# State outputs in four column quarters, mLSTM gate rows transposed beside the second chunk, NSA weights between second and third chunk

## The chip, the cores and the metric

One core of one Trainium2 chip runs the whole program in one launch. The metric is the time on the device in microseconds, the median of several runs. The other seven cores do nothing.

## The reference, cut to what matters

The program is two layers on 256 tokens of width 2048, all float32. The first layer has three branches: stick-breaking attention (8 heads), an S5 state space layer (64 groups, here 8 blocks of four state tiles) and an mLSTM (4 heads), then a mixture of 32 experts. The second layer has an RG-LRU branch, NSA attention (8 heads) and a forgetting attention. Three pieces bear on the change.

```python
# S5: the output of the states, 8 groups' 128 channels per block
y = einsum('bsgp,ghp->bsgh', states, c_mat).real + d_skip * u
# mLSTM: gates per head and token, used by row and by column
log_f = log_sigmoid(f_pre); b = cumsum(log_f)
log_d = b[t] - b[s] + log_i[s]
# NSA: probabilities of softmaxes over keys, then the values
p = masked_softmax(q @ k.T * scale, mask)
o = gate * (p @ v)
```

## The kernel before, in words

Activations lie with channels on the 128 partitions and the 256 tokens along the free axis. Every weight matrix comes in chunks of one megabyte (128 x 2048 floats). SyncE issues their loads into four buffers `stage`. ScalarE copies a chunk to `w_hi` (fp32r), GpSimd computes the rest `w_lo` = stage - w_hi in four pieces of 512 columns (L549), and TensorE (`chunk`, `wide`) multiplies: 32 matmuls with w_hi, then 16 with w_lo, into bank k of `acc`, chunk n using bank n mod 4. GpSimd's `low` for chunk n waits until chunk n - 2 is done, for `w_lo` has two buffers. `wide` takes a function `mid` that is called between the 32 and the 16 matmuls, and that is where small products of an earlier head are put. `opening` multiplies the first tiles of a projection whose last tile isn't computed yet, `closing` the rest. `evac_done` counts the evacuations of acc.

The engines run their own programs and meet in semaphores only; the order of work on each is the order in the code. Loops over heads are software pipelined: iteration i projects head i (g) and computes head i - 1 (s).

`stage_a` (attention and S5). Its projections are `plain`: 32 fp32 records from `stage` directly, chunks 0 to 3 giving q, k, v, u; a function passed in is called ahead of t = 11 of 16. A product in fp32 is two records of TensorE. Around them stand the scores and transposes of v; `bu(j)`, the input of state tile j into bank 2 of `wk`, for j = 0 to 3; `sums`; `values`; and `cmm(j)`, the product of the rotated states of tile j with their output matrix `A_cm`, 32 output channels, which go to partitions 32j to 32j + 31 of bank 3 of `wk`. On VectorE, `rotate(j)` turns bu(j) into the states: t1 and t2 from bank 2, vr, two scans (A_sc), t1 and t2 again, and `srot`; its two buffers are reused, so rotate(2) and (3) wait for cmm(0) and (1). The order on VectorE is rotate(0), sp, rotate(1), the argument of w, rotate(2), the mask of w, rotate(3), yl, y5 (which waits for the last cmm), then `tables` of the next head, from which ScalarE computes sine and cosine. GpSimd has no work in this stage until its end. After the eighth head the first chunks of projection p_sb are opened beside what is left of it; their w_hi are copied by ScalarE behind the softplus of the eighth head.

`ada_part` multiplies 512 columns by 32 columns in each of four quarters of the array, as the expert stage (`up_step`, `down`) does with four experts.

mLSTM gates. Chunk `mlif` gives the gates of all heads; ScalarE evacuates them, converts one more w_hi and computes abs, exp, ln; VectorE follows with six steps (row_d 1 to 6) on four partitions. TensorE waits for them (L835), transposes rows to columns (L837), waits for `row_done`, and runs the eight chunks of head 0 (`stage_b(0, None)`, beside which no head's products stand). ScalarE waits for `row_t` ahead of its part of stage_b.

`stage_c` (NSA, one RG-LRU block beside each head) has four chunks per head. TensorE runs `scores`, chunk 0, chunk 1 with `probs` as its mid, chunk 2 with `values` as its mid, chunk 3. `probs` begins with `sums` of the next head, then waits for the scaled weights of VectorE (c_d, C_P) and transposes them (L1142, L1144); ScalarE copies the transposed ones to SBUF (C_pT, C_pcT) for `values`.

Of the kernel before, what the change touches and what calls it, by code (L numbers as in the profile page):

```python
# [22 lines left out]
P = 128  # L23
T = 256
# [84 lines left out]
def build(nc, dr):  # L109
# [37 lines left out]
    M0 = D0 + 32768  # L147
# [35 lines left out]
    A = {}  # L183
# [5 lines left out]
    for n, s in [("ph", [P, 4, T]), ("sin", [P, 4, T]), ("cos", [P, 4, T]), ("t1", [P, 2, T]), ("t2", [P, 2, T])]:  # L189
        A[n] = ar("A_" + n, s)  # L190
    ar = Area(S0, END)
    for n, s in [("y5", [P, WT, T]), ("vr", [P, 2, T]), ("sc", [P, 2, T]), ("srot", [P, 2, 2, T]),
                 ("craw", [P, 4, 2, 32]), ("cm", [P, 4, 2, 32]), ("c1", [P, 4, 2, 32]), ("c2", [P, 4, 2, 32]),
                 ("mask", [P, 2, T]), ("iota", [P, T]), ("s5p", [P, 14, 32])]:
        A[n] = ar("A_" + n, s)
    ar = Area(S0 + 8192, S0 + 8192 + 6144)
# [368 lines left out]
    def _(pe):  # L565
# [179 lines left out]
        def stage_a(g, s):  # L745
# [10 lines left out]
            def cmm(j):  # L756
                rs = slice(32 * j, 32 * j + 32)
                pe.wait_ge(srot_ready, s * 4 + j + 1)
                mm(wk[rs, 3, 0:T], A["cm"][:, j, 0, :], A["srot"][:, j % 2, 0, :], True, False)
                mm(wk[rs, 3, 0:T], A["cm"][:, j, 1, :], A["srot"][:, j % 2, 1, :], False, True)\  # L760
                    .then_inc(cmm_done, 1)
# [34 lines left out]
            if s is not None:  # L796
                pe.wait_ge(vtok_ready, s + 1)
                cmm(0)
                bu(2)
            if g is not None:  # L800
                plain(2, g)
            else:
                opening("p_sb", 2, 7)
            if s is not None:
                cmm(1)
                bu(3)
                values()
            beside_plain(3, g, s, lambda: cmm(2))
            if s is not None:
                cmm(3)  # L810
# [24 lines left out]
        pe.wait_ge(row_d, 6)  # L835
        for st in range(2):
            last = pe.transpose(wk[:, 0, 4 * st:4 * st + 4], B["g"][0:4, st * P:(st + 1) * P], ident[0:4, 0:4])  # L837
        last.then_inc(row_t, 1)
        pe.wait_ge(row_done, 1)
        base_b = BASE["ml"]  # L840

        def stage_b(g, s):
# [18 lines left out]
            for j in range(8):  # L861
                if g is not None:
                    wide(*slot(base_b + j, g, 2))
                elif j < 4:
                    opening("p_ml", j, 6)
# [12 lines left out]
        stage_b(0, None)  # L878
        with pe.Fori(1, 4) as i:
            stage_b(i, i - 1)  # L880
# [228 lines left out]
        def stage_c(g, s, kv):  # L1109
# [26 lines left out]
            def probs():  # L1136
                if g is not None:
                    sums()
                pe.wait_ge(c_d, s * NC_D + (C_FIRST + C_P))
                for i in range(2):  # L1140
                    for st, tt in ((0, 0), (0, 1), (1, 1)):
                        pe.transpose(wk[:, i, (st + tt) * P:(st + tt + 1) * P], C["z"][:, 2 * i + tt, st * P:(st + 1) * P], ident[:])  # L1142
                for tt in range(2):
                    last = pe.transpose(wk[0:16, tt, 384:512], C["zc"][:, tt, :], ident[:])  # L1144
                last.then_inc(c_p, 1 if g is not None else 2)
# [23 lines left out]
            beside(base_c + 1, g, s, probs, "p_a", 1)  # L1169
# [671 lines left out]
    def _(dve):  # L1841
# [156 lines left out]
        def stage_a(g, s):  # L1998
# [20 lines left out]
            def rotate(j):  # L2019
# [23 lines left out]
                if j >= 2:  # L2043
                    dve.wait_ge(cmm_done, s * 4 + j - 1)
                tt(A["srot"][:, j % 2, 0, :], A["t1"][:, 0, :], A["t2"][:, 1, :], SUB)
                tt(A["srot"][:, j % 2, 1, :], A["t2"][:, 0, :], A["t1"][:, 1, :], ADD).then_inc(srot_ready, 1)
# [17 lines left out]
            dve.wait_ge(cmm_done, s * 4 + 4)  # L2064
# [817 lines left out]
```

## Time and profile before

| | us |
|---|---|
| median of 3 runs | 3269.16 (3265.61 to 3270.73) |
| profiled execution, on the device | 3263.18 |
| its span | 3261.4 |
| TensorE busy | 2918.5 (89%) |
| GpSimd busy | 1677.4 (51%) |
| VectorE busy | 1270.4 (39%) |
| ScalarE busy | 1183.5 (36%) |
| mean granted TensorE clock | 0.957 of full speed |

Rows of the profile name an engine (PE is TensorE, PEld its weight load, DVE VectorE, ACT ScalarE, POOL GpSimd, SP SyncE), a line of the kernel, the operation and the tiles (written <- read). Starts are in microseconds from the span's start. A bracket such as [1.63 <-DVE C_rq] is idle time of the engine just before, and what ended it. Matmuls overlap: the time of a merged row runs to the end of its last record, and the next row begins before that. Most lines are those of helpers (L567 is `mm`, L1843 VectorE's `tt`, L1287 ScalarE's `fn`), so groups are told apart by their tiles. The heads of stage_a lie between 130 and 415 us, the mLSTM gates at 820, the NSA heads between 2172 and 2415.

### The profile page before, as it was taken

To read this page: it belongs to the slowest core of one execution; us is meant where nothing else is said; L and a number is where in the kernel's file an instruction comes from. 1 tells how busy PE (TensorE), PEld (TensorE's weight loads), DVE (VectorE), ACT (ScalarE), POOL (GpSimd) and SP (SyncE) were. 2 spreads that over 40 slices of the span, in tenths; PEclk is the share of its full clock that TensorE was granted. 3 is DMA by queue.
4 is the path that set the end of the run, shared out by engine and by line. 5 is a ranking of instruction groups with operands and counts; after the bars stand their busy time and mean duration, and the time that the engine had idled before them with its cause. 6 is when DMAs were issued, how large, how long until landed. Compare 5 with 4: busy or idle time off the path is not lost.

```text
span 3261.4 us, 51720 instructions
## 1 busy us (share of the span) xinstructions
PE 2918.5 (89%) x20048; PEld 2413.4 (74%) x20048; DVE 1270.4 (39%) x2025; ACT 1183.5 (36%) x1378; POOL 1677.4 (51%) x1274
## 2 busy tenths in 40 slices
PE   6899979999899999857788768979999999999998
PEld 1677767787898878733344427879988989999998
DVE  1477742214363252331222214436633153324335
ACT  1222233333445332310111104546554446654343
POOL 0000047677677676400000003966669997769798
PEclk8999989999999999978999988989999999999999
DMA  9533337558344586659777893543335554445444
GB/s 390 205 109 109 109 112 287 199 217 296 133 151 158 182 305 249 223 209 414 328 321 314 333 420 148 191 140 138 132 131 193 182 195 155 154 142 193 158 168 142
DMA packets 98628, 679.77 MB, mean 208 GB/s; under 512 B 11584, under 2 KB 15424, under 8 KB 16832
## 3 DMA queue, kind: packets, MB, share of 16 engines
q1 hardware_dynamic: 83088, 602.97, 49.4%
q10 hardware_dynamic: 15408, 74.85, 6.1%
q8 instruction: 106, 1.74, 0.2%
q14 instruction: 26, 0.21, 0.0%
HBM read 770.05 MB, written 2.10 MB: 237 GB/s over the span
## 4 chain that ended last, share of the span: by engine, by line
PE 70%; DMA 12%; DVE 6%; ACT 5%; issue 3%; POOL 2%; ACTq 1%; SPq 1%; DVEq 0%; POOLq 0%
PE acc L567 42%; PE wk L567 11%; PE acc L640 9%; DMA ring<-in_moe 6%; PE acc L644 5%; DMA side_buf<-in_ada 3%; POOL w_lo L549 2%; DMA stage<-in_ada 2%; PE acc L653 2%; ACT L1287 1%; ACT w_hi L1287 1%; DVE C_z L1846 1%; DMA stage<-in_main 1%; SPq L499 1%; ACT hb L1287 0%
## 5 line engine op out<-in xcount | busy, mean ns | idle before, releaser
L549 POOL TENSOR_TENSOR w_lo<-stage,w_hi 128x512 fp32r<-128x512 f32 x1268 | 1670.2, 1351 | 1535.3 <-ACT w_hi L1287 1014.3
L1287 ACT ACTIVATE w_hi<-stage 128x2048 fp32r<-128x2048 f32 x317 | 603.8, 1907 | 47.9 <-DMA stage<-in_main 47.5
L567 PE MATMUL acc<-xhl,w_hi 128*128 128x256 f32 x4064 | 525.2, 288 | 21.9 <-DVE xhl L1843 9.8
L567 PEld LDWEIGHTS acc<-xhl,w_hi 128*128 128x128 f32 x4064 | 509.2, 196 | 25.9 <-DVE xhl L1843 6.8
L640 PE MATMUL acc<-xhl,w_hi 128*128 128x512 f32 x1536 | 371.3, 394 | 0.0
L640 PEld LDWEIGHTS acc<-xhl,w_hi 128*128 128x128 f32 x1536 | 281.6, 188 | 92.7 <-issue 37.7
L567 PE MATMUL acc<-xhl,w_lo 128*128 128x256 f32 x2032 | 274.6, 289 | 2.0 <-POOL w_lo L549 2.0
L567 PEld LDWEIGHTS acc<-xhl,w_lo 128*128 128x128 f32 x2032 | 259.3, 196 | 5.5 <-issue 2.5
L567 PE MATMUL acc<-h,stage 128*128 128x256 f32 x1024 | 232.8, 384 | 2.9 <-ACT h L1287 2.9
L567 PEld LDWEIGHTS acc<-h,stage 128*128 128x128 f32 x1024 | 193.5, 191 | 38.3 <-issue 12.8
L567 PE MATMUL acc<-ring,xg 128*32 128x512 f32 x1024 | 145.2, 712 | 73.0 <-DMA ring<-in_moe 72.3
L644 PEld LDWEIGHTS acc<-xhl,w_lo 128*128 128x128 f32 x1536 | 196.9, 191 | 7.5
L644 PE MATMUL acc<-xhl,w_lo 128*128 128x256 f32 x1536 | 199.1, 283 | 0.0
L1287 ACT ACT_TABLE_LOAD x137 | 175.8, 1283 | 51.3 <-DVE G_sg L1843 27.4
L567 PEld LDWEIGHTS acc<-ring,xg 128*32 128x32 f32 x1024 | 41.5, 128 | 170.8 <-issue 169.9
L567 PE MATMUL acc<-yh,w_hi 128*128 128x256 f32 x576 | 141.6, 284 | 5.2 <-DVE yl L1843 5.2
L567 PE MATMUL acc<-yl,w_hi 128*128 128x256 f32 x576 | 141.2, 283 | 0.0
L567 PE MATMUL acc<-dh,w_hi 128*128 128x256 f32 x512 | 127.2, 289 | 6.4 <-DVE dl L1843 6.4
L567 PE MATMUL acc<-dl,w_hi 128*128 128x256 f32 x512 | 125.3, 285 | 0.0
L1843 DVE TENSOR_TENSOR X_hid<-X_s,acc 128x256 f32<-128x256 f32 (+1 forms) x12 | 5.0, 418 | 297.3 <-ACT X_s L1287 297.3
L567 PEld LDWEIGHTS acc<-yh,w_hi 128*128 128x128 f32 x576 | 109.8, 191 | 5.5 <-DVE yl L1843 3.6
L567 PEld LDWEIGHTS acc<-dh,w_hi 128*128 128x128 f32 x512 | 98.6, 193 | 19.3 <-issue 16.2
(485 smaller groups left out, 4054.2 us busy)
## 6 DMA issues: line engine op xcount, KB each, us to landing
stage<-in_main SPq DMA_DIRECT2D x317, 1024.0 KB, 4.8
ring<-in_moe SPq DMA_DIRECT2D x192, 1024.0 KB, 10.4
side_buf<-in_ada ACTq DMA_DIRECT2D x64, 1024.0 KB, 5.0
over_lo<-in_moe ACTq DMA_DIRECT2D x48, 1024.0 KB
over_hi<-in_moe ACTq DMA_DIRECT2D x42, 1024.0 KB
stage<-in_ada SPq DMA_DIRECT2D x32, 1024.0 KB, 8.6
stage<-in_sb SPq DMA_DIRECT2D x32, 1024.0 KB, 4.8
x<-in_x ACTq DMA_DIRECT2D x1, 2048.0 KB, 12.9
```

What stands on the lines that cost most here:

```text
L499: sp.dma_start(ring[:, r, :], dr["moe"][tile * 6 + c]).then_inc(ring_in[r], 16)
L549: last = pool.tensor_tensor(w_lo[:, k % 2, cs], stage[:, k, cs], w_hi[:, k, cs].bitcast(F32), ALU.subtract)
L567: return pe.matmul(o, w, r, start=start, stop=stop)
L640: pe.matmul(acc[:, k, :], w_hi[:, k, t * P:(t + 1) * P], xhl[:, :, t, :], start=t == 0, stop=False, skip_group_check=True)
L644: last = pe.matmul(acc[:, k, 0:T], w_lo[:, k % 2, t * P:(t + 1) * P], xh[:, t, :], start=False, stop=t == DT - 1, skip_group_check=True)
L653: return pe.matmul(o, w, r, start=start, stop=stop, skip_group_check=True)
L1287: return act.activation(o, i, f, **kw)
L1843: return dve.tensor_tensor(o, a, b, op)
L1846: return dve.tensor_scalar(o, a, s1, s2, op0, op1) if op1 else dve.tensor_scalar(o, a, s1, None, op0)
```

## The change

1. `cmm` is one block of eight matmuls for all four tiles, with the quarter j running fastest, called ahead of t = 11 of the fourth projection (or in the middle of the fourth opening), after a wait for all four rotations. `srot` has four buffers (the two new ones lie where sq1 was), so rotate waits for no cmm. `bu(3)` moves from behind the third projection into it, and y5 waits for cmm_done s + 1.
2. `columns` (the wait for the gate rows and their two transposes) is the mid of the second mLSTM chunk; the wait for row_done is behind all eight chunks of head 0.
3. In stage_c `sums` is the mid of chunk 1 by itself, and `probs` stands between chunks 1 and 2.

```diff
--- before.py
+++ after.py
@@ -188,11 +188,13 @@
     ar = Area(M0, S0)
     for n, s in [("ph", [P, 4, T]), ("sin", [P, 4, T]), ("cos", [P, 4, T]), ("t1", [P, 2, T]), ("t2", [P, 2, T])]:
         A[n] = ar("A_" + n, s)
+    srots = [None, None, sb("A_srot2", [P, 2, T], at=M0), sb("A_srot3", [P, 2, T], at=M0 + 2048)]
     ar = Area(S0, END)
     for n, s in [("y5", [P, WT, T]), ("vr", [P, 2, T]), ("sc", [P, 2, T]), ("srot", [P, 2, 2, T]),
                  ("craw", [P, 4, 2, 32]), ("cm", [P, 4, 2, 32]), ("c1", [P, 4, 2, 32]), ("c2", [P, 4, 2, 32]),
                  ("mask", [P, 2, T]), ("iota", [P, T]), ("s5p", [P, 14, 32])]:
         A[n] = ar("A_" + n, s)
+    srots[0], srots[1] = A["srot"][:, 0], A["srot"][:, 1]
     ar = Area(S0 + 8192, S0 + 8192 + 6144)
     for n, s in [("y5sg", [P, 2, 2 * T]), ("sg", [P, 2, T])]:
         A[n] = ar("A_" + n, s)
@@ -753,12 +755,14 @@
                 mm(wk[:, 2, 0:T], A["bcur"][rs, 0, :], A["u"][rs, :])
                 mm(wk[:, 2, T:2 * T], A["bcur"][rs, 1, :], A["u"][rs, :]).then_inc(bu_done, 1)
 
-            def cmm(j):
-                rs = slice(32 * j, 32 * j + 32)
-                pe.wait_ge(srot_ready, s * 4 + j + 1)
-                mm(wk[rs, 3, 0:T], A["cm"][:, j, 0, :], A["srot"][:, j % 2, 0, :], True, False)
-                mm(wk[rs, 3, 0:T], A["cm"][:, j, 1, :], A["srot"][:, j % 2, 1, :], False, True)\
-                    .then_inc(cmm_done, 1)
+            def cmm():
+
+                pe.wait_ge(vtok_ready, s + 1)
+                pe.wait_ge(srot_ready, s * 4 + 4)
+                for c in range(2):
+                    for j in range(4):
+                        last = mm(wk[32 * j:32 * j + 32, 3, 0:T], A["cm"][:, j, c, :], srots[j][:, c, :], c == 0, c == 1)
+                last.then_inc(cmm_done, 1)
 
             if s is not None:
                 pe.wait_ge(sb_evac, s * 4 + 7)
@@ -794,20 +798,11 @@
                 bu(1)
             beside_plain(1, g, s, sums)
             if s is not None:
-                pe.wait_ge(vtok_ready, s + 1)
-                cmm(0)
                 bu(2)
-            if g is not None:
-                plain(2, g)
-            else:
-                opening("p_sb", 2, 7)
+            beside_plain(2, g, s, lambda: bu(3))
             if s is not None:
-                cmm(1)
-                bu(3)
                 values()
-            beside_plain(3, g, s, lambda: cmm(2))
-            if s is not None:
-                cmm(3)
+            beside_plain(3, g, s, cmm)
 
         heads(pe, stage_a)
 
@@ -832,11 +827,13 @@
 
         each(pe, BASE["mlif"], 1, wide)
         ada_columns(3, side_row[1])
-        pe.wait_ge(row_d, 6)
-        for st in range(2):
-            last = pe.transpose(wk[:, 0, 4 * st:4 * st + 4], B["g"][0:4, st * P:(st + 1) * P], ident[0:4, 0:4])
-        last.then_inc(row_t, 1)
-        pe.wait_ge(row_done, 1)
+
+        def columns():
+            pe.wait_ge(row_d, 6)
+            for st in range(2):
+                last = pe.transpose(wk[:, 0, 4 * st:4 * st + 4], B["g"][0:4, st * P:(st + 1) * P], ident[0:4, 0:4])
+            last.then_inc(row_t, 1)
+
         base_b = BASE["ml"]
 
         def stage_b(g, s):
@@ -860,7 +857,7 @@
                 last.then_inc(bvt_done, 1)
             for j in range(8):
                 if g is not None:
-                    wide(*slot(base_b + j, g, 2))
+                    wide(*slot(base_b + j, g, 2), mid=columns if j == 1 and s is None else None)
                 elif j < 4:
                     opening("p_ml", j, 6)
                 if j == 1 and s is not None:
@@ -876,6 +873,7 @@
                     last.then_inc(num_done, 1)
 
         stage_b(0, None)
+        pe.wait_ge(row_done, 1)
         with pe.Fori(1, 4) as i:
             stage_b(i, i - 1)
         pe.wait_ge(by_ready, 3)
@@ -1134,8 +1132,6 @@
                 last.then_inc(c_p, 1)
 
             def probs():
-                if g is not None:
-                    sums()
                 pe.wait_ge(c_d, s * NC_D + (C_FIRST + C_P))
                 for i in range(2):
                     for st, tt in ((0, 0), (0, 1), (1, 1)):
@@ -1166,7 +1162,11 @@
                 wide(*slot(base_c, g))
             else:
                 opening("p_a", 0, 7)
-            beside(base_c + 1, g, s, probs, "p_a", 1)
+            if g is not None:
+                wide(*slot(base_c + 1, g), mid=sums)
+            else:
+                opening("p_a", 1, 7)
+            probs()
             beside(base_c + 2, g, s, values, "p_a", 2)
             if g is not None:
                 wide(*slot(base_c + 3, g))
@@ -2040,10 +2040,8 @@
                 tt(A["t1"][:], A["sc"][:], cos, MUL)
                 tt(A["t2"][:], A["sc"][:], sin, MUL).then_inc(vo_ch, 1)
                 dve.wait_ge(vo_ch, done.next())
-                if j >= 2:
-                    dve.wait_ge(cmm_done, s * 4 + j - 1)
-                tt(A["srot"][:, j % 2, 0, :], A["t1"][:, 0, :], A["t2"][:, 1, :], SUB)
-                tt(A["srot"][:, j % 2, 1, :], A["t2"][:, 0, :], A["t1"][:, 1, :], ADD).then_inc(srot_ready, 1)
+                tt(srots[j][:, 0, :], A["t1"][:, 0, :], A["t2"][:, 1, :], SUB)
+                tt(srots[j][:, 1, :], A["t2"][:, 0, :], A["t1"][:, 1, :], ADD).then_inc(srot_ready, 1)
 
             rotate(0)
 
@@ -2061,7 +2059,7 @@
             rotate(3)
             dve.wait_ge(yh_ready, s + 1)
             tt(yl[:, s, :], wk[:, 0, 0:T], yh[:, s, :].bitcast(F32), SUB).then_inc(yl_ready, 1)
-            dve.wait_ge(cmm_done, s * 4 + 4)
+            dve.wait_ge(cmm_done, s + 1)
             tt(A["y5"][:, s, :], wk[:, 3, 0:T], A["du"][:], ADD).then_inc(y5_ready, 1)
             done.check()
             if g is not None:
```

## Rows read from the trace of the kernel before

**Rows 1.** the page, part 1 (busy, share, count) and part 4 (chain)
```profile
PE 2918.5 (89%) x20048; PEld 2413.4 (74%) x20048; DVE 1270.4 (39%) x2025; ACT 1183.5 (36%) x1378; POOL 1677.4 (51%) x1274
...
PE 70%; DMA 12%; DVE 6%; ACT 5%; issue 3%; POOL 2%; ACTq 1%; SPq 1%; DVEq 0%; POOLq 0%
```

**Rows 2.** waits of TensorE, whole span: total us, times, longest
```profile
PE acc L653 <- ACT w_hi L1287: 12.9, 1, 12.9
...
PE wk L1142 <- DVE C_rq L1846: 11.6, 7, 1.8
...
PE wk L837 <- DVE B_rows L1849: 10.6, 1, 10.6
...
PE wk L567 <- DVE A_t L1843: 3.2, 6, 0.5
...
PE wk L1142 <- DVE C_zc L1846: 0.7, 1, 0.7
```

**Rows 3.** timeline of TensorE in a head: start, us, what, count
```profile
370.04 1.05 PE L567 MATMUL wk<-A_srot,A_cm 128*32 128x256 f32 x4
...
371.02 2.43 PE L567 MATMUL acc<-h,stage 128*128 128x256 f32 x10
```

**Rows 4.** timeline of VectorE in the heads
```profile
342.25 0.69 DVE L1843 TENSOR_TENSOR A_t<-wk,A_cos 128x512 f32<-128x512 f32 x1 [0.17 <-ACT A_cos L1287]
...
364.34 0.69 DVE L1843 TENSOR_TENSOR A_t<-wk,A_cos 128x512 f32<-128x512 f32 x1 [2.86 <-PE wk L567]
...
369.20 0.76 DVE L1843 TENSOR_TENSOR A_srot<-A_t,A_t 128x256 f32<-128x256 f32 x2
...
374.55 0.42 DVE L1843 TENSOR_TENSOR A_y<-wk,A_du 128x256 f32 x1 [4.25 <-PE wk L567]
...
415.34 0.42 DVE L1843 TENSOR_TENSOR A_y<-wk,A_du 128x256 f32 x1 [4.26 <-PE wk L567]
```

**Rows 5.** timeline of TensorE behind the heads
```profile
430.44 0.55 PE L653 MATMUL acc<-yh,w_hi 128*128 128x256 f32 x1 [12.89 <-ACT w_hi L1287]
...
459.23 1.05 PE L567 MATMUL wk<-A_srot,A_cm 128*32 128x256 f32 x4
```

**Rows 6.** timeline of TensorE: quarters in ada_part, and in the experts
```profile
806.11 1.06 PE L567 MATMUL wk<-side_buf,cact 128*32 128x512 f32 x8 [0.58 <-DMA side_buf<-in_ada]
...
1702.99 3.64 PE L567 MATMUL acc<-ring,xg 128*32 128x512 f32 x32
```

**Rows 7.** timeline of TensorE around the mLSTM gates
```profile
819.74 0.95 PE L567 MATMUL wk<-ident,side_row 128*128 128x4 f32 x8
...
831.32 0.37 PE L837 MATMUL wk<-ident,B_rg 4*128 4x4 f32 x2 [10.63 <-DVE B_rows L1849]
...
839.13 4.00 PE L567 MATMUL acc<-xhl,w_hi 128*128 128x256 f32 x32
...
842.97 2.08 PE L567 MATMUL acc<-xhl,w_lo 128*128 128x256 f32 x16
```

**Rows 8.** timeline of VectorE there: the gate chain's first step
```profile
828.22 0.41 DVE L1849 SCALAR_TENSOR_TENSOR B_rlf<-B_rlf,B_rl 4x256 f32<-4x256 f32 x1 [7.31 <-ACT B_rl L1287]
```

**Rows 9.** timeline of GpSimd there
```profile
839.44 5.48 POOL L549 TENSOR_TENSOR w_lo<-stage,w_hi 128x512 fp32r<-128x512 f32 x4 [14.46 <-PE acc L567]
```

**Rows 10.** windows: busy (count) by engine, granted clock, DMA share, GB/s
```profile
825.00:830.00 5.00, 0.00 (x0) 0.00 (x0) 1.68 (x4) 3.08 (x4) 0.00 (x0) 0.50 0.64 210
```

**Rows 11.** tile B_rm: duration ns min/median/max, first and last start
```profile
L1846 DVE TENSOR_SCALAR B_rm<-B_rows,ident x4: 470/1508/1508, 862.4 to 1034.3; 4x512 f32<-4x512 f32 x4
```

**Rows 12.** timeline of TensorE in an NSA head
```profile
2281.63 0.50 PE L567 MATMUL wk<-ones,C_qs 128*128 128x1 f32 x4
...
2283.75 0.88 PE L1142 MATMUL wk<-ident,C_z 128*128 128x128 f32 x6 [1.63 <-DVE C_rq L1846]
...
2290.43 0.59 PE L567 MATMUL wk<-C_pT,C_vtok 128*128 128x256 f32 x2
```

**Rows 13.** timeline of ScalarE there
```profile
2284.88 0.81 ACT L1287 ACTIVATE C_pT<-wk 128x768 f32<-128x768 f32 x1 [0.58 <-PE wk L1144]
```

## Prediction

> **What bounds the kernel now.** I read the page's busy times and chain first: TensorE is busy 89% of the span and carries 70% of the chain that ended last [rows 1]. So a microsecond is won where TensorE has less to do or stops waiting, and the list of TensorE's waits says where it waits [rows 2]. Five of its lines belong to the three places of this change: 3.2 us in six waits on A_t, one of 12.9 us on w_hi behind the heads, one of 10.6 us on B_rows ahead of the mLSTM chunks, 11.6 us in seven waits on C_rq and one of 0.7 us on C_zc in the NSA heads. That is 39 us of waiting, besides the work that the first edit packs closer. Then I read the timelines around each.
>
> **State outputs in quarters (stage_a).** Removed on TensorE: the four separate cmm blocks of a head. One block is two fp32 matmuls, four records, from 370.04 to 371.02: 0.98 us [rows 3], which is 4 x 0.216 (ten of the next kind take 2.43 to the end of the last) and a switch of 0.1. Added: one block of eight matmuls, 16 records, in which four neighbours go to four column quarters. What do neighbours in different quarters cost? The trace has them: ada_part's eight records of 512 columns (four quarters, twice) take 1.06 us to the end of the last, and 32 such records in the expert stage 3.64 us; the 24 more cost 2.58, 0.107 us each, where a record of 512 columns by itself needs 2 x 0.216 = 0.43 [rows 6]. Four run at once. With 256 columns a round of four costs 0.216, and the new block has four rounds: 0.87 + 0.1 = about 0.98 us. The bounds: 0.98, and serial 16 x 0.216 + 0.1 = 3.56. I take 0.98, since ada_part is the same form. The Trainium skill ("TensorE: Matmul & The Clock Gate", measured speedup) gives three column tiles a speedup of 2.38 and four row tiles 3.07, not 4. By 3.07, an estimate, the block would cost 1.2 and the sum below would be 1.8 us smaller; the expert row, at its full fourfold rate, speaks against it.
>
> Three blocks fewer in a head is 2.94 us. From the first full head to the end of the last projection of the eighth, 27 old blocks become 7 new ones: 20 x 0.98 = 19.6 us. What could eat it is the new wait for all four rotations, behind which the last ten projection matmuls, the next scores and everything else on TensorE queue up. Before, the last rotation ran 364.34 to 369.96 (5.62 us), after VectorE had sat idle 2.86 us for the fourth bu [rows 4]. That bu moves ahead of the end of the third projection, so VectorE no longer waits and the rotation ends at 367.1. TensorE gets to the place of the new block at 370.04 less two old blocks, 368.1: 1.0 us to spare, and more later, since y5 (before at 374.55) now follows at 369.2 and the tables with it. The 0.53 us wait on A_t goes too: rotation 0 begins 8.5 us after y5 (342.25, where the y5 before it was at 333.76, one period of 40.79 us ahead of 374.55; the period is 415.34 less 374.55, [rows 4]), reads its product by 379.0 (two steps, 0.69 us each, [rows 4]), and TensorE asks for that at 380.9 (before at 383.9; three blocks, 2.94, earlier). 6 waits: 3.2 us. The loads of the next S5 matrices (ScalarE's queue, behind the values' evacuation and the fourth bu) come forward with both; stage's projection loads are a megabyte each in 9 us or more. No new wait there. VectorE's own loop from y5 to y5 is 8.5 + 4 x 5.6 + 2.6 for the three mask steps + 1.1 = 34.6 us under a period of 37.3.
>
> The end of the heads: y5 of the seventh head at 415.34 [rows 4] starts tables, sine, softplus, the copies of w_hi, and TensorE begins p_sb at 430.44 after 12.9 us idle [rows 5]. That chain now starts 2.35 us before the end of the last projection instead of 0.98 us behind it: 3.3 us less idle. Then the openings, counted from the first one's start: the first takes 7.5 us, bu 1 1.0, the second with sums 6.5, and without cmm 0 bu 2 ends at 16.1. Rotation 2 and the mask step end at 22.3; the third opening (3.3) with bu 3 inside ends at 20.4, so values wait 1.9 us and end at 23.4. Rotation 3 ends at 27.9; half of the fourth opening (1.7) is done at 25.1, so the block waits 2.7 and ends at 28.9, and the other half at 30.5. Before, all was done 0.98 us behind 459.23, at 29.8 from 430.44 [rows 5]: 0.7 us lost. Behind it the GpSimd w_lo chain starts at the first closing and moves along. Part one: 19.6 + 3.2 + 3.3 - 0.7 = 25.4 us.
>
> **mLSTM gate columns (columns).** Before: ada_columns end at 820.65 (819.74 + 0.9), TensorE is idle to 831.32, transposes, waits for row_done, has chunk 0 issued at 839.13 and chunk 1 at 844.9 (842.97 and 16 x 0.12) [rows 7]: 24.3 us. The granted clock fell to 0.50 in the idle, the 1.2 GHz level [rows 10], and so chunk 0 took longer than chunk 1's 5.76 us. After: chunk 0 (5.76), the first 32 of chunk 1's 48 matmuls (3.84, from 839.13 to 842.97 before), then the wait at 830.25. The gate chain on ScalarE and VectorE is unmoved and would be ready at 831.3, a wait of 1.0. But now a GpSimd w_lo of four pieces, that began at 839.44 when chunk 0 was done [rows 9], begins at 826.6 and lies over the VectorE chain, six steps from 828.22 on [rows 8]. What such overlap costs, a step on four partitions shows: 0.47 us alone, 1.51 beside GpSimd [rows 11]. Between nothing and 0.9 us on each step; the w_lo ends about 832.0, so the chain ends about 833.6: wait 3.3 us. The Trainium skill ("GPSIMD Engine Reference", key points) names this contention for VectorE instructions with two SBUF inputs or in a 2-port mode; by it both scans suffer as well, which changes nothing as w_lo's end limits it. After the wait: transposes and switches 0.4, last 16 matmuls 1.95; end 835.9. Gain 9.0 us (between 8, when the clock falls in the wait, and 11.3, with no contention). ScalarE stands in its wait for row_t, so chunk 0's evacuation and the next w_hi come at 834 instead of 826.8; that w_hi is for chunk 4, wanted at 845 or later. row_done, now behind eight chunks, is free. A stage buffer is released by w_lo, not by this, so loads hold.
>
> **NSA weights (stage_c).** Before: sums at 2281.63, then an idle of 1.63 us, the transposes of C_z at 2283.75 [rows 12]. After: sums 0.36 at the same place, then the chunk's 16 w_lo matmuls (1.95), then the transposes at about 2284.05; VectorE's weights were ready at 2283.70. The wait is gone with 0.3 us to spare; the extra switch costs 0.1. The values need ScalarE's copies: they begin at 2284.88 [rows 13], take 0.81 and a small one, and end some 1.3 us behind the transposes, and TensorE now gets to values 3.84 us behind them instead of 5.8 (2290.43, [rows 12]): held. Chunk 1 is done 2.5 us earlier, so its w_lo partner lies over VectorE's LRU steps, perhaps 3 us longer; those are wanted only after values, and the next conv starts at the third chunk's evacuation, 8 us off. Gain 7 x (1.66 - 0.1) = 10.9, and 0.6 in the last head, where the 0.7 us on C_zc goes: 11.5.
>
> **Sum.** 25.4 + 9.0 + 11.5 = 45.9 us. The profiled execution took 3263.18 us on the device for a span of 3261.4, 6.0 under the median of the three runs, 3269.16; so 3217.3 for an execution like it, and 3223 against the median, which I forecast. What lies behind the three places moves as a block: the expert stage's ring loads are released by chunks, not by a clock of their own.
>
> **Rivals.**
> Quarters don't overlap in this form (the eight matmuls accumulate in one bank, two rounds over). For it: no row has 256 columns in quarters. Against: the expert rows accumulate round after round. Then 2.6 us more in each of seven heads: 3241. Chance 0.12.
> A wait only moves. In NSA the spare is 0.3 us; were VectorE's scaling a microsecond or two later, the wait would come back at the new place: 11 us kept, 3234. Chance 0.10. With the first case, or with the mLSTM gain lost too, 3250: 0.05.
> More than I count: no GpSimd overlap in the gate chain, a clock that holds through the openings: 3217 or a little less. Chance 0.10.
> The other side: VectorE's loop becomes the bound. All rotations now lie between cmm and cmm without overlap by the next y5. It decides from 37.3 us on (34.6 by rows), and makes the kernel slower only from about 43.7 us a head, that is with VectorE's steps a quarter longer; then 3276. For it: GpSimd overlap does such things. Against: GpSimd is idle in this stage. Chance 0.03.
> The change does nothing measurable (waits reappear in full, quarters serial): 3266, chance 0.04.
> The forecast itself: 0.56.
>
> **How the numbers follow.** The forecast's own bounds (the block 0.98 to 1.2, the gates 8 to 11.3, runs that spread by 5 us) give 3215 to 3230. With the serial and the NSA case the range is 3209 to 3245; beyond it are at most 0.12. A measurement of this kernel tells 0.2%, 6.5 us, from no change. Faster by more: 0.93; within: 0.04; slower: 0.03.
>
> **What would show it.** In the profile after: the x16 group wk<-A_srot,A_cm of about 1.1 us once a head with no idle before it; period 37.3; no wait on A_t; p_sb's opening about 26 us earlier; the L837 transposes behind an idle of 1 to 4 us and a clock of 1.00 in chunk 0; the L1142 transposes with no idle, and values with none. A block of 3.5 us, an idle ahead of it, or an idle ahead of the values would make it wrong.

## The result, and the profile after

The kernel after takes 3214.33 us (median of 4 runs, 3209.77 to 3221.9), beside 3268.67 for the kernel before in the same rounds: a ratio of 0.9839 with a 95% interval of 0.9823 to 0.9854, about 54 us less. Forecast were 3223 with a range of 3209 to 3245; the result lies in the range, and just below the forecast's own bounds of 3215 to 3230. The profiled execution took 3212.35 us on the device for a span of 3210.6, 50.8 less than the span of before, so the forecast of 3217.3 for such an execution was 5 us too high.

The page, parts 1 and 4, and then TensorE's waits over the whole span (total us, times, longest), those that answer to [rows 1, 2]:

```profile
PE 2891.5 (90%) x20048; PEld 2402.3 (75%) x20048; DVE 1291.0 (40%) x2025; ACT 1182.6 (37%) x1378; POOL 1682.0 (52%) x1274
...
PE 55%; DMA 9%; DVE 4%; ACT 2%; issue 2%; POOL 2%; SPq 1%; ACTq 1%; DVEq 0%; POOLq 0%
```

```profile
PE acc L655 <- ACT w_hi L1287: 10.8, 1, 10.8
...
PE wk L834 <- DVE B_rows L1849: 3.7, 1, 3.7
...
PE wk L569 <- DVE A_srot L1843: 2.7, 1, 2.7
...
PE wk L569 <- DVE A_w L1843: 1.5, 1, 1.5
```

TensorE has as many instructions as before and 27 us less busy time. Some 23.5 of them are the blocks: eight heads have three blocks of 0.98 us fewer each, since records in different quarters now lie over each other. The rest is not split up; the clock has a part in it, for matmuls at the lower clock are busy longer. The waits on A_t, C_rq and C_zc are gone, B_rows is 3.7 instead of 10.6. I cut the trace at TensorE instructions that both kernels have: heads are first to eighth scores (wk<-A_q,A_k), "to p_sb" from there to the first matmul on yh, "p_sb" from there to the next product of a side buffer, "gates" from the second transposes of side_row to the first product of B_qk, "NSA" first to eighth wk<-C_ks,C_q. The remainder is all else; most of it is stages that wait for loads, and it holds the eighth NSA head too. All in us (the difference is taken before rounding):

| kernel | heads | to p_sb | p_sb | gates | NSA | remainder | span |
|---|---|---|---|---|---|---|---|
| before | 284.9 | 15.3 | 72.4 | 63.9 | 223.4 | 2601.6 | 3261.4 |
| after | 259.5 | 13.1 | 73.5 | 58.0 | 208.0 | 2598.4 | 3210.6 |
| difference | 25.3 | 2.2 | -1.1 | 5.9 | 15.4 | 3.2 | 50.8 |

The heads of after. Timeline of TensorE, start, us, what, count; first a block of quarters one head earlier, then one with what is next to it:

```profile
349.76 1.07 PE L569 MATMUL wk<-A_srot,A_cm 128*32 128x256 f32 x16
...
386.83 1.07 PE L569 MATMUL wk<-A_srot,A_cm 128*32 128x256 f32 x16
387.83 2.43 PE L569 MATMUL acc<-h,stage 128*128 128x256 f32 x10
```

Sixteen records take 1.00 us from the block's start to the next row's, no idle is in front of them, and the period is 37.07 us. In before four records took 0.98, about the same [rows 3]. The block has room: on VectorE the last rotation of the first of these two heads ends at 347.65, 2.1 us ahead of the block, where 1.0 was forecast.

```profile
346.89 0.76 DVE L1843 TENSOR_TENSOR A_srot<-A_t,A_t 128x256 f32<-128x256 f32 x2
```

The gates. Timelines of TensorE, VectorE and GpSimd, then windows (length, then busy us and count of PE, PEld, DVE, ACT and POOL, then granted clock, DMA share, GB/s):

```profile
792.30 4.07 PE L569 MATMUL acc<-xhl,w_hi 128*128 128x256 f32 x32
...
798.12 4.00 PE L569 MATMUL acc<-xhl,w_hi 128*128 128x256 f32 x32
805.82 0.37 PE L834 MATMUL wk<-ident,B_rg 4*128 4x4 f32 x2 [3.69 <-DVE B_rows L1849]
806.12 3.78 PE L569 MATMUL acc<-xhl,w_lo 128*128 128x256 f32 x16
809.70 5.07 PE L569 MATMUL acc<-xhl,w_hi 128*128 128x256 f32 x32
```

```profile
799.98 1.28 DVE L1849 SCALAR_TENSOR_TENSOR B_rlf<-B_rlf,B_rl 4x256 f32<-4x256 f32 x1 [7.33 <-ACT B_rl L1287]
801.29 1.66 DVE L2116 TENSOR_TENSOR_SCAN B_rb<-ones,B_rlf 4x256 f32<-4x256 f32 x1
...
804.32 0.68 DVE L2120 TENSOR_TENSOR_SCAN B_rm<-ones,B_rg 4x256 f32<-4x256 f32 x1
```

```profile
798.44 5.58 POOL L551 TENSOR_TENSOR w_lo<-stage,w_hi 128x512 fp32r<-128x512 f32 x4 [1.59 <-PE acc L569]
```

```profile
800.00:803.00 3.00, 2.12 (x18) 1.92 (x16) 2.93 (x3) 0.00 (x0) 3.00 (x3) 1.00 0.38 161
803.00:806.00 3.00, 0.18 (x2) 0.18 (x2) 2.66 (x4) 0.00 (x0) 1.01 (x1) 0.88 0.31 44
806.00:809.00 3.00, 3.00 (x15) 2.98 (x15) 2.05 (x6) 2.18 (x2) 0.00 (x0) 0.50 0.73 309
809.00:812.00 3.00, 3.00 (x16) 3.00 (x15) 1.61 (x2) 2.07 (x2) 2.02 (x2) 0.50 0.02 5
```

Up to 804.0 GpSimd's w_lo lies over VectorE's chain: the first step takes 1.28 us where it took 0.41 [rows 8], and the scans are 1.66 beside GpSimd and 0.68 behind it. That makes most of the wait of 3.69 us (gates_hold, below). The Trainium skill ("GPSIMD Engine Reference", key points) names VectorE instructions with two SBUF inputs or in a 2-port mode for this contention. The scans and the first step have two, and the trace agrees. In gates_third a step that reads one tile, the TENSOR_SCALAR on B_rows, is drawn out too, from 0.28 to 1.20 us; whether it runs in such a mode no run shows. Behind the wait the clock is 0.50 for 6 us: 16 w_lo matmuls take 3.78 us, not the 2.08 of [rows 7], and the next 32 take 5.07, not 4.00.

NSA in after, timeline of TensorE: no idle ahead of the transposes, none ahead of the values.

```profile
2241.81 0.50 PE L569 MATMUL wk<-ones,C_qs 128*128 128x1 f32 x4
2242.17 2.15 PE L569 MATMUL acc<-xhl,w_lo 128*128 128x256 f32 x16
2244.16 0.82 PE L1138 MATMUL wk<-ident,C_z 128*128 128x128 f32 x6
...
2248.86 0.59 PE L569 MATMUL wk<-C_pT,C_vtok 128*128 128x256 f32 x2
```

### The profile page after: what moved, and what is told of

It is laid out like the page before. It is cut to its first block, busy times and chain, and to the rows that moved or that the text cites. A ratio compares the mean times of both kernels' runs of the same rounds, so it can differ in the third digit from the quotient of the medians.

```text
span 3210.6 us, 51704 instructions
## 1 busy us (share of the span) xinstructions
PE 2891.5 (90%) x20048; PEld 2402.3 (75%) x20048; DVE 1291.0 (40%) x2025; ACT 1182.6 (37%) x1378; POOL 1682.0 (52%) x1274
## 4 chain that ended last, share of the span: by engine, by line
PE 55%; DMA 9%; DVE 4%; ACT 2%; issue 2%; POOL 2%; SPq 1%; ACTq 1%; DVEq 0%; POOLq 0%
PE acc L569 35%; DMA ring<-in_moe 8%; PE wk L569 7%; PE acc L642 7%; PE acc L646 4%; POOL w_lo L551 2%; DMA side_buf<-in_ada 2%; PE acc L655 2%; ACT w_hi L1287 1%; SPq L501 1%; ACT hb L1287 0%; DVE hb L1843 0%; ACT L1287 0%; DMA stage<-in_main 0%; DVE dl L1843 0%
```

## The experiments

**Each edit alone.** The first three kernels have one part of the diff each, on top of the kernel before (the first is the change of `cmm`, `srots` and `stage_a`; the second that of the mLSTM `columns`; the third that of `stage_c`).

The core of each:

```diff
-            beside_plain(3, g, s, lambda: cmm(2))
-            if s is not None:
-                cmm(3)
+            beside_plain(3, g, s, cmm)
```

> The kernel before with the first edit alone (the one block in four quarters, bu(3) moved, four srot buffers). Theory: the block costs about 1.0 us and the A_t wait is gone, so a head takes 37.1 us instead of 40.8, the opening of p_sb comes 27 us earlier and the whole gains 25 to 28 us: 3241 to 3244 against 3268.7. Rival (a part of the gain is given back in the side-loaded stages behind, which wait for DMA): under 20 us in the whole, though the heads are 26 us shorter.

```diff
-                    wide(*slot(base_b + j, g, 2))
+                    wide(*slot(base_b + j, g, 2), mid=columns if j == 1 and s is None else None)
```

> The kernel before with the gate columns in the second mLSTM chunk alone. Prediction on record: 9.0 us. Theory from the two traces: TensorE's wait of 3.7 us is followed by about 6 us at the 1.2 GHz level, which costs 2.8 us, so the stretch from ada_columns to the first B_qk product is 5.9 us shorter and the whole gains 4 to 8 us. Rival: the clock fell in that one execution by chance; then here the wait is followed by a clock of 1.00 and the stretch is 8.7 us shorter.

```diff
-            beside(base_c + 1, g, s, probs, "p_a", 1)
+            if g is not None:
+                wide(*slot(base_c + 1, g), mid=sums)
+            else:
+                opening("p_a", 1, 7)
+            probs()
```

> The kernel before with the NSA edit alone. Prediction on record: 10.9 us for seven heads, 11.5 in all. Theory from the two traces: 1.76 us a head, and two heads of the kernel before (34.3 and 32.9 us instead of 31.2) lost 3.1 and 1.7 us more after their waits, by the clock, which goes too: heads of 29.5 us, 15 us in all. Rival: those two long heads have another cause and stay: 12.3 us in all.

| kernel | median, us | ratio to before (95%) | heads | to p_sb | p_sb | gates | NSA | remainder |
|---|---|---|---|---|---|---|---|---|
| p1_only | 3247.69 | 0.9934 (0.9917 to 0.9951) | 259.5 | 13.1 | 75.5 | 64.1 | 223.4 | 2604.9 |
| p2_only | 3262.37 | 0.9976 (0.9962 to 0.9990) | 284.8 | 15.3 | 72.0 | 57.6 | 223.4 | 2617.4 |
| p3_only | 3248.98 | 0.9937 (0.9918 to 0.9956) | 284.8 | 15.3 | 72.0 | 64.6 | 208.0 | 2603.3 |

Each edit moves its own stretch, by what it moves it in the whole change to 0.4 us, and no other (gates differ by up to 0.7 us without a cause known, and p_sb is in question to 3 us). Within that the parts are independent, as the sum assumed. In p2_only the wait of 3.69 us and the 3.78 us of w_lo behind it are there again, so the fall of the clock was no accident of one execution.

The whole times say less. Against the median of the kernel before in their rounds, 3269.61, p1_only is 21.9 us faster, where 25 to 28 were expected and its stretches give 24; p2_only is 7.2, within the 4 to 8 expected; p3_only is 20.6, where its stretch gives 15.4. The remainder, whose code is the same in all but for the eighth NSA head, lies between 2597 and 2617 us over thirteen profiled executions. A single edit of 6 us is read from its stretch, not from a median of a few runs (ten of p2_only, four of the others).

**Are the quarters at once, and what for?** Two kernels on top of after, one with another order of the block's matmuls, one with the block done twice:

```diff
-                for c in range(2):
-                    for j in range(4):
+                for j in range(4):
+                    for c in range(2):
```

> The changed kernel, with the eight state-output matmuls of a head in another order: both matmuls of a quarter one behind the other, then the next quarter, where the changed kernel goes through the four quarters and then once more. Theory: matmuls run at once only where neighbours in the stream are in different quarters. Then two records out of four have a neighbour of their own quarter ahead (each matmul being two records, half and half), the block of 16 records, 1.01 to 1.07 us in the changed kernel, takes from 2.0 us (pairs serial) to 3.5 us (all serial), the period of a head goes from 37.08 to 38.1 to 39.6 us, and the kernel becomes 7 to 20 us slower than the changed kernel's 3214. Rival: each matmul starts when its quarter is free, whatever stands in front of it, with its two halves already one behind the other in the same quarter: the block stays at about 1.0 us and the time at 3214.

```diff
-                for c in range(2):
+                for c in (0, 1, 0, 1):
```

> The changed kernel, with the eight state-output matmuls of a head done twice (the second pass starts the sums anew, so what is computed stays the same): 32 records where there were 16. Theory: four quarters at once and TensorE the bound of a head: the block goes from 1.01 to 1.07 us to 1.88 (0.87 more), the period of a head from 37.08 to 37.95, and the kernel from 3214 to 3221. Rival (VectorE's loop bounds the head by now, so that TensorE has slack behind the block): the block grows and the period stays at 37.1. Rival (quarters are partly serial and the short block hides it in a fixed share): the block goes to more than 2.2 us.

Timelines of TensorE, the first fence of the other order, the second of the doubled block:

```profile
386.26 1.09 PE L569 MATMUL wk<-A_srot,A_cm 128*32 128x256 f32 x16
387.28 2.43 PE L569 MATMUL acc<-h,stage 128*128 128x256 f32 x10
```

```profile
356.35 1.93 PE L569 MATMUL wk<-A_srot,A_cm 128*32 128x256 f32 x32
...
394.30 1.93 PE L569 MATMUL wk<-A_srot,A_cm 128*32 128x256 f32 x32
396.16 2.43 PE L569 MATMUL acc<-h,stage 128*128 128x256 f32 x10
```

Then two windows of the other order, of the block's records alone (length, busy and count of TensorE, clock, DMA share, GB/s):

```profile
386.26:386.32 0.06, 0.06 (x4) 1.00 0.00 0
386.32:386.48 0.16, 0.16 (x4) 1.00 0.00 0
```

The first theory, that only neighbours in different quarters overlap and the block takes 2.0 to 3.5 us, fell; its rival held. With all four records of a quarter one behind another the block takes 1.02 us from start to start, 0.02 more, and the heads 259.7 us instead of 259.5 (3218.71 us, ratio 0.9847, 0.9827 to 0.9866). So the matmuls needn't alternate between quarters within 16 records. The windows show how it starts: four records within the first 0.06 us, and no fifth up to 0.22. The trace doesn't name the quarter of a record. But records of one quarter alone started 0.216 us apart in before [rows 3], so the four are most likely in four quarters, and three of them then began ahead of earlier records of a busy quarter. How TensorE does that is not shown.

The doubled block takes 1.86 to 1.87 from start to start, 0.87 more as expected: four more rounds of 0.216. The period is 37.95, so the block is on the path to the full and VectorE's loop has at least 0.9 us to spare. The heads are 265.6 us, 6.0 more, about 7 x 0.87 (3223.79 us, ratio 0.9875, 0.9857 to 0.9894).

**The gates: what makes the wait, and what the clock?** Three kernels on top of after. The first puts the transposes one chunk later:

```diff
-                    wide(*slot(base_b + j, g, 2), mid=columns if j == 1 and s is None else None)
+                    wide(*slot(base_b + j, g, 2), mid=columns if j == 2 and s is None else None)
```

> The kernel after with the gate columns as the mid of the third mLSTM chunk instead of the second. Theory: TensorE comes to the columns 5.8 us later, when the rows are ready or nearly so, so the 3.7 us wait goes and with it the low clock behind it (2.8 us): 5 to 6.5 us shorter from ada_columns to the first B_qk product than in the kernel after. Rival (ScalarE, which stands in its wait for the columns, becomes late with the w_hi of the fifth chunk): a new wait on w_hi of 1 us or more at the fifth chunk, and a gain under 4 us.

The second holds GpSimd back until the six VectorE steps are done:

```diff
-        each(pool, 4, BASE["kv"] - 4, low)
+        each(pool, 4, BASE["ml"] + 2 - 4, low)
+        pool.wait_ge(row_d, 6)
+        each(pool, BASE["ml"] + 2, BASE["kv"] - BASE["ml"] - 2, low)
```

> The changed kernel, with the first low-part subtraction of the third mLSTM chunk on GpSimd held until the six VectorE steps of the gate chain are done. Theory: the wait of 3.7 us on B_rows is GpSimd's contention with VectorE's steps, and the clock of 0.50 behind it comes of the wait: with GpSimd held the steps take about 0.3 to 0.7 us each as before the change, the wait is about 1.0 us, the clock stays at 1.00, the 16 low matmuls behind it take 2.08 instead of 3.78 and the high ones 4.00 instead of 5.07: the stretch from the gates' side row to the first B_qk matmuls goes from 58.0 to about 52.5 to 53 us. The third chunk's low part is then ready at about 5.6 us behind the end of the chain, 0 to 1 us ahead of TensorE's need. Rival (the steps wait for something else than GpSimd, ScalarE's chain say): the wait stays at 3 us or more and the clock falls again. Rival (the wait moves): a new wait of 1 to 4 us on w_lo at the third chunk, and the stretch ends where it was.

The third leaves GpSimd and the wait as they are and keeps TensorE occupied ahead of it:

```diff
         def columns():
+            for _ in range(14):
+                mm(wk[:, 0, T:T + P], ones[:], ident[:])
             pe.wait_ge(row_d, 6)
```

> The changed kernel with 14 extra 128-column matmuls (ones by the identity, into a part of the bank that nobody reads; some 3.0 us in all) on TensorE right ahead of its wait for the gate rows, of 3.7 us in the changed kernel. The wait itself stays. Theory: the clock of 0.50 behind the wait comes of TensorE standing idle; filled, the idle is 0.7 us, the clock stays at 1.00, the 16 low matmuls behind it take 2.1 us instead of 3.78 and the next 32 take 4.0 instead of 5.07, and the stretch from the side row to the first B_qk matmuls goes from 58.0 to 55.3. Rival: the clock falls for another reason (the load on the other engines at that time, or a fixed moment of the program): the low matmuls stay at 3.78, the stretch at 58.0.

gates_hold, timeline of VectorE, then of TensorE:

```profile
802.32 0.41 DVE L1851 SCALAR_TENSOR_TENSOR B_rlf<-B_rlf,B_rl 4x256 f32<-4x256 f32 x1 [7.32 <-ACT B_rl L1289]
802.77 0.68 DVE L2118 TENSOR_TENSOR_SCAN B_rb<-ones,B_rlf 4x256 f32<-4x256 f32 x1
803.48 0.41 DVE L1845 TENSOR_TENSOR B_rg<-B_rli,B_rb 4x256 f32<-4x256 f32 x1
```

```profile
805.42 0.28 PE L836 MATMUL wk<-ident,B_rg 4*128 4x4 f32 x2 [0.95 <-DVE B_rows L1851]
805.63 2.18 PE L571 MATMUL acc<-xhl,w_lo 128*128 128x256 f32 x16
```

gates_filled, timeline of TensorE, then a window of it:

```profile
804.57 3.29 PE L569 MATMUL wk<-ident,ones 128*128 128x128 f32 x28
808.43 0.28 PE L836 MATMUL wk<-ident,B_rg 4*128 4x4 f32 x2 [0.57 <-DVE B_rows L1851]
808.64 2.18 PE L569 MATMUL acc<-xhl,w_lo 128*128 128x256 f32 x16
```

```profile
806.00:809.00 3.00, 2.43 (x22) 2.22 (x21) 2.44 (x5) 0.20 (x1) 0.63 (x1) 1.00 0.24 82
```

| kernel | wait on B_rows | w_lo x16 behind it | gates | median, us | ratio to before (95%) |
|---|---|---|---|---|---|
| after | 3.69 | 3.78 | 58.0 | 3214.33 | 0.9839 (0.9823 to 0.9854) |
| gates_third | 0.85 | 2.18 | 52.4 | 3216.46 | 0.9842 (0.9817 to 0.9866) |
| gates_hold | 0.95 | 2.18 | 53.5 | 3213.44 | 0.9844 (0.9823 to 0.9866) |
| gates_filled | 0.57 | 2.18 | 55.3 | 3217.7 | 0.9842 (0.9821 to 0.9862) |

gates_hold: with GpSimd held, all six steps are at their short durations and the wait is 0.95 instead of 3.69 us. GpSimd's overlap makes 2.7 us of the wait. The rival that the wait would move is right for a part, though not at w_lo. The first product of B_qk comes 1.1 us later than in gates_third, since it waits 2.75 us for ScalarE's evacuation and not 1.77. ScalarE's w_hi copies ahead of it wait 2.2, 2.0, 3.3 and 1.4 us for loads, where those of gates_third don't; that the stage buffers come free later behind the held w_lo is the likely reason, not tested. Another 1.5 us goes behind that product (170.4 us from the first to the fourth, 168.9 in every other kernel), and the trace says on what: behind the idle of 2.75 us the clock is 0.50 and the eight matmuls take 3.43 us, behind the one of 1.77 it is 1.00 and they take 1.99. Timeline and window, first of gates_hold, then of gates_third:

```profile
847.35 3.43 PE L571 MATMUL wk<-B_qk 128*128 128x256 f32 x8 [2.75 <-ACT B_qk L1289]
847.00:849.00 2.00, 1.65 (x4) 1.38 (x5) 0.00 (x0) 1.58 (x2) 1.31 (x2) 0.50 0.38 160
...
843.15 1.99 PE L569 MATMUL wk<-B_qk 128*128 128x256 f32 x8 [1.77 <-ACT B_qk L1287]
843.00:845.00 2.00, 1.85 (x8) 1.44 (x8) 0.00 (x0) 1.38 (x2) 1.25 (x2) 1.00 0.00 0
```

gates_filled tells the clock: the gate rows come no earlier than in after, TensorE merely isn't idle, the clock stays at 1.00 and the stretch is 2.7 us shorter, which is what 16 + 32 matmuls at the lower clock had cost (3.78 less 2.18, and 5.07 less 4.00). So of after's gate stretch 5.6 us can be had, as gates_third shows: 2.8 of the wait and 2.7 of the clock behind it. In none of the three does the median show that, by the remainder's spread above.

**The kernel itself again, and a version that takes more.** hi_early is gates_third with the first copy of p_sb's w_hi moved ahead of the softplus on ScalarE:

```diff
             if s is not None:
+                if g is None:
+                    high(0, 0)
                 act.wait_ge(zm_ready, s + 1)
...
-                    for k in range(4):
+                    for k in range(1, 4):
```

> The changed kernel with the gates' transposes one chunk later (as in gates_third: stretch 52.4 us instead of 58.0) and, at the end of the S5 heads, the first of the four high-part copies of the next projection ahead of the softplus on ScalarE instead of behind it, where TensorE waits 10.8 us for the first. Theory: TensorE waits for that one copy: the wait goes from 10.8 to about 5 us, the stretch from the last scores to that projection from 13.1 to about 8, and all in all the kernel is 8 to 11 us faster than the changed kernel: 3204 to 3207. Rival: the softplus and with it w come 1 us later, and the second to fourth copies too, so the wait moves to the openings behind (A_w 1.5 us now): then the gain is 5 to 7 us, 3207 to 3210, all of it the gates'. Rival: the gain at the gates is eaten by the stages that wait for loads, as a single comparison of gates_third left open: 3214.

> The changed kernel itself, once more, as the baseline of the next two and to see how far the stages that wait for loads move from one execution to the next. Expected: 3210 to 3218 us; stretches without load waits (heads 259.5, gates 58.0, NSA heads 208.0) the same to 0.3 us; the stretches with loads each within 6 us of before.

> The kernel of hi_early once more (gates' transposes one chunk later, first high-part copy ahead of the softplus), now beside the changed kernel in the same rounds. Its own stretches were 5.6 us (gates) and 4.8 (softplus) shorter, its median 1 us lower than the changed kernel's of another call. Theory: both gains are real on TensorE and are kept: 5 to 10 us under after_again. Rival: the stages behind, which wait for loads, give the time back, since the loads don't start earlier by as much: within 3 us of after_again, and the sum of the stretches p_sb to first B_qk and B_qk to the end shows where.

hi_early: 3213.36 us (ratio 0.9838, 0.9823 to 0.9852). That misses the 3204 to 3207 of its theory and the 3207 to 3210 of the moved wait; the 3214 of the third case, a gain eaten by the stages that wait for loads, is the nearest. In the rounds with both, after_again 3218.47 us (0.9847, 0.9829 to 0.9864) and hi_early_again 3215.01 (0.9834, 0.9816 to 0.9851), 3.5 us less, between the 5 to 10 of the theory and the 3 of its rival. after_again lies 0.5 us above the 3218 that it was given; its stretches without loads are the same to 0.1 us, as expected. Stretches of the profiled executions:

| kernel | heads | to p_sb | p_sb | gates | NSA | remainder | span |
|---|---|---|---|---|---|---|---|
| after | 259.5 | 13.1 | 73.5 | 58.0 | 208.0 | 2598.4 | 3210.6 |
| after_again | 259.5 | 13.1 | 74.6 | 57.9 | 208.0 | 2606.9 | 3220.0 |
| hi_early | 259.5 | 8.3 | 77.7 | 52.4 | 208.0 | 2596.7 | 3202.6 |
| hi_early_again | 259.5 | 8.3 | 77.6 | 52.4 | 208.0 | 2608.2 | 3214.0 |

TensorE's waits of hi_early from 390 to 440 us:

```profile
PE acc L655 <- ACT w_hi L1287: 6.0, 1, 6.0
PE acc L655 <- POOL w_lo L551: 5.3, 2, 4.0
PE wk L569 <- DVE A_srot L1845: 2.7, 1, 2.7
PE wk L569 <- DVE A_sp L1845: 1.9, 1, 1.9
PE wk L569 <- DVE A_w L1845: 1.4, 1, 1.4
```

The wait on w_hi is 4.8 us shorter, as expected, but the openings behind stop where they did not: 1.9 us for A_sp and 1.3 us for the first w_lo. From the first matmul on yh to the values of the last head it is 26.9 us (397.85 to 424.76) against 22.75 in after (403.16 to 425.91). Of 4.8 us 4.2 are given back at once, 3.2 of them in these two waits: the rival of the moved wait. In the second pair of executions 3.0 are given back (p_sb 77.6 against 74.6). What is left is the 5.6 of the gates and 0.6 to 1.8. The ten runs of hi_early have a median of 3213.6 us, the nine of the kernel after 3217.5: 3.9 us less, with a standard error of some 1.8 (standard deviations 3.4 and 4.3). It has the lowest median of the versions run, but the difference is 0.1% and some two standard errors, and the four runs of gates_hold (3213.44) are not told apart from it.

## Why the prediction was right, point by point

**Quarters.** The block was to cost 0.98 us and costs 1.00, against bounds of 0.98 and 3.56; the rival of serial quarters is out, and so is VectorE's loop as the bound. The Trainium skill ("TensorE: Matmul & The Clock Gate", measured speedup) gives a speedup of 3.07 for four row tiles and 2.38 for three column tiles. Neither is this form, and the measurement is higher: the doubled block shows 0.216 for a round of four, and the four records of one quarter in before took 0.216 each too, which makes 4. The steps that were too small are the price of the wait and that of a block. I took 20 blocks off up to the end of the last projection and six waits of 0.53, 22.8 us; the 21st block, the last of the seventh head, was in the 3.3 us of the end of the heads. As I cut the stretches it belongs to the heads, so the forecast for them is 23.8, and 2.3 for the end. Starts of the scores in before, timeline of TensorE:

```profile
130.29 1.03 PE L567 MATMUL wk<-A_q,A_k 128*128 128x256 f32 x4
170.39 1.13 PE L567 MATMUL wk<-A_q,A_k 128*128 128x256 f32 x4
211.18 1.13 PE L567 MATMUL wk<-A_q,A_k 128*128 128x256 f32 x4
```

The first period of before is 40.10 us and has no wait on A_t, the next are 40.79: a wait that shows as 0.53 cost 0.69. And 40.10 against the 37.08 of after is 3.0 for three blocks, not 2.94. So 7 x 3.0 and 6 x 0.7 are 25.2, measured 25.3, 1.5 more than forecast. The end of the heads gave 2.2 us against 2.3. The openings took 1.1 us more, not 0.7; their waits came at 1.5 and 2.7 us, where 1.9 and 2.7 were forecast. Part one is 26.4 us against 25.4.

**mLSTM gates.** The forecast wait was 3.3 us, measured 3.7, for the reason given (gates_hold). The failed term is what comes behind it. I had the clock's fall in the range (8 us as the lower bound) but let it cost 1 us; it costs 2.7 (gates_filled), and the part gives 5.9 us, not 9.0, outside its own bounds. Chunk 0 ran at 1.00 as forecast. The forecast of 9.0 had no term for what an idle does to the matmuls after it, though [rows 10] shows the level that it leaves.

**NSA.** The gap went and no wait took its place; the rival that it moves is out. Forecast were 10.9 us over seven heads, measured 15.4. A plain head went from 31.22 to 29.47 us, 1.75 instead of 1.56: 12.3 us. The rest is clock again. Timeline of TensorE in the first head of before, then a window in it:

```profile
2188.60 0.87 PE L1142 MATMUL wk<-ident,C_z 128*128 128x128 f32 x6 [1.62 <-DVE C_rq L1846]
2189.32 0.38 PE L1144 MATMUL wk<-ident,C_zc 128*16 128x128 f32 x2
2189.45 3.32 PE L567 MATMUL acc<-xhl,w_lo 128*128 128x256 f32 x16
```

```profile
2189.50:2192.50 3.00, 3.00 (x18) 3.00 (x17) 2.45 (x7) 1.06 (x2) 0.00 (x0) 0.58 0.86 322
```

Behind two of the seven idles of before the clock fell (w_lo x16 in 3.32 and 3.56 us, not 2.08), and these heads took 34.33 and 32.93 us. In after it stays up; its first head takes 31.10, 1.63 over the others, with a wait of 1.37 on C_uc that before has too. So 3.1 + 1.7 - 1.6 = 3.2 us, and with 12.3 it is 15.5. I read one head and took it for all; a list of the starts would have shown the long ones. The traces of p1_only and p2_only, which have the same seven idles, show two falls each as well, and the same 223.4 us for the heads. But there they stand behind the second and the fifth idle, where in before it was the first and the fifth. The fifth, at 1.8 us the longest, is among them each time. Why the clock falls behind these and not behind the others stays open.

**Sum.** 26.4 + 5.9 + 15.4 = 47.7 us against 45.9, and the remainder gave 3.2 more, which is within its spread. The two errors of the clock, 3 us too much at the gates and 3 too little in NSA, cancelled, and that was luck. The median came out 9 us under 3223. The stretches explain 1.8 of them and the remainder 3.2. The other 4 are not of the change: the median of before that I started from was 6.0 us above its profiled execution, and that of after is 2.0 above its own. That the time comes near the 3217 or less of the rival with no GpSimd overlap does not speak for it; the overlap and the fall of the clock were there.

## What to carry to other kernels

Small outputs of 32 rows that are done one behind another cost four times what they cost in one block of four quarters (4 x 0.98 us against 1.00 here); what it takes is that all inputs are ready at one place, so buffers for them and a place behind the last. An idle of TensorE of 1.6 to 3.7 us is to be priced with what follows it: in this kernel 1.4 to 2.7 us more, where the clock fell. Where a wait can't be avoided, put it one piece of work later, or fill it. And where stages that wait for loads swing by 10 us, compare stretches of the trace between instructions that both kernels have.

## What the runs showed of the hardware

- Four quarters of 32 columns run at once even if all matmuls of a quarter stand one behind another: 16 records in 1.02 us, against 1.00 in turns.
- Small VectorE steps on four partitions beside GpSimd's subtractions are drawn out to about GpSimd's own rhythm (5.58 us for four pieces, 1.4 each): 0.41 to 1.28, and a scan 0.68 to 1.66 (after and gates_hold). A TENSOR_SCALAR that reads one tile is drawn out too: 0.28 to 1.20 (gates_hold and gates_third).
- A fall of the clock to 0.50 behind an idle of 3.7 us lasted 6 us and cost 2.7; filling the idle with useless matmuls kept it at 1.00 (gates_filled). Behind an idle of 2.75 us it fell and cost 1.4 (gates_hold), behind one of 1.77 at the same place it stayed (gates_third). Behind idles of 1.6 and 1.8 us in the NSA heads it fell in two of seven cases (before, p1_only, p2_only).
